# Mixing layers of a two-stack transformer kernel: VectorE's weight splits moved behind the maxima, ScalarE's split apart from them, and two scores put ahead of two value products

## What is computed

```python
h = rms_norm(x, attn_norm[l])
proj = h @ w_in[l]                       # 1024 x 2720, in column blocks of 256
o_a = neighborhood_attention(...)        # 4 heads, bias per row
o_b = diff_attention(...)                # 4 heads, two softmaxes each: p1 - lam * p2, then rms_norm
o_c = dilated_attention(...)             # 4 heads, bias
o_d = mla_attention(...)                 # 4 heads, 96 features
x = x + concatenate([o_a, o_b, o_c, o_d]) @ w_o[l]
```

## Time and profile before

| | |
|---|---|
| median of 3 runs | 1145.87 us (1145.69 to 1145.92) |
| the profiled execution's own time | 1145.93 us |
| its span, first to last instruction | 1143.9 us |
| TensorE busy | 1130.8 us, 99% of the span |
| VectorE busy | 778.2 us, 68% |
| ScalarE busy | 535.6 us, 47% |
| TensorE's granted clock, mean | 0.998 |

### The profile page before, as it was taken

One profiled execution on the slowest core, in us unless ns is written; L12 is line 12 of the kernel. 1 busy time (PEld: TensorE's weight loads), 2 busy tenths in 40 slices (PEclk: granted clock), 3 DMA queues, 4 the chain that ended last, 5 costly groups with the idle time before them and its releaser, 6 DMA issues. The chain is left out here.

```text
span 1143.9 us, 17037 instructions
## 1 busy us (share of the span) xinstructions
PE 1130.8 (99%) x6662; PEld 982.6 (86%) x6662; DVE 778.2 (68%) x999; ACT 535.6 (47%) x704; POOL 32.8 (3%) x47
## 2 busy tenths in 40 slices
PE   9999999999999999999999999999999999999997
PEld 7888888898888888879988888888899888888886
DVE  6766666766667666677686676666766866766665
ACT  5533333456653333344576543343446755433332
POOL 0000000000000000003000000000030000000000
PEclk9999999999999999999999999999999999999999
DMA  8765556764346555658423465556673243665550
GB/s 277 243 208 198 179 204 200 225 201 148 111 166 221 185 193 181 212 146 268 147 100 111 166 221 183 185 184 209 178 232 111 75 136 127 218 207 196 182 186 37
DMA packets 167131, 204.57 MB, mean 179 GB/s; under 512 B 19988, under 2 KB 150028, under 8 KB 167078
## 3 DMA queue, kind: packets, MB, share of 16 engines
q1 hardware_dynamic: 166606, 203.11, 54.6%
q10 hardware_dynamic: 472, 0.73, 0.2%
HBM read 202.66 MB, written 1.16 MB: 178 GB/s over the span
## 5 line engine op out<-in xcount | busy, mean ns | idle before, releaser
L628 ACT ACTIVATE whi<-raw 128x2048 fp32r<-128x2048 f32 x176 | 336.4, 1914 | 382.7 <-PE bank L1516 245.5
L949 DVE TENSOR_TENSOR wlo<-raw,whi 128x2048 fp32r<-128x2048 f32 x171 | 391.9, 2293 | 163.4 <-ACT whi L628 163.3
L1512 PE MATMUL bank<-h_both,whi 128*128 128x512 f32 x1280 | 304.6, 390 | 0.0
L1512 PEld LDWEIGHTS bank<-h_both,whi 128*128 128x128 f32 x1280 | 237.7, 188 | 47.7
L1486 PE MATMUL bank<-whi,o_hi 128*128 128x512 f32 x448 | 176.3, 393 | 0.0
L1487 PE MATMUL bank<-wlo,o_hi 128*128 128x512 f32 x448 | 174.9, 390 | 0.0
L1488 PE MATMUL bank<-whi,o_lo 128*128 128x512 f32 x448 | 174.4, 389 | 0.0
L1516 PEld LDWEIGHTS bank<-h_both,wlo 128*128 128x128 f32 x1280 | 164.1, 191 | 6.2
L1516 PE MATMUL bank<-h_both,wlo 128*128 128x256 f32 x1280 | 166.0, 283 | 0.0
L1488 PEld LDWEIGHTS bank<-whi,o_lo 128*128 128x128 f32 x448 | 84.1, 188 | 17.9
L1486 PEld LDWEIGHTS bank<-whi,o_hi 128*128 128x128 f32 x448 | 84.3, 188 | 17.6 <-issue 1.3
(11 more groups left out here) (179 smaller groups left out, 1172.6 us busy)
## 6 DMA issues: line engine op xcount, KB each, us to landing
raw<-in_w_gate_up SPq DMA_DIRECT2D x44, 1024.0 KB, 5.0
raw<-in_w_down SPq DMA_DIRECT2D x44, 1024.0 KB, 4.8
raw<-in_w_gate SPq DMA_DIRECT2D x22, 1024.0 KB, 5.1
raw<-in_w_up SPq DMA_DIRECT2D x22, 1024.0 KB, 5.1
raw<-in_w_in SPq DMA_DIRECT2D x20, 1024.0 KB, 6.2
raw<-in_w_o SPq DMA_DIRECT2D x12, 1024.0 KB, 4.8
raw<-in_w_kv SPq DMA_DIRECT2D x8, 1024.0 KB, 5.4
raw<-in_w_q SPq DMA_DIRECT2D x4, 1024.0 KB, 5.4
```

The costliest lines, as they stand in the source:

```text
L628: act.activation(whi[:, s, :], raw[:, s, :], ACT.Copy).then_inc(hi_ready, 1)
L949: dve.tensor_tensor(wlo[:, s, :], raw[:, s, :], whi[:, s, :].bitcast(F32), ALU.subtract).then_inc(lo_ready, 1)
L1512: pe.matmul(bank[bk + jj][:, :], hi[:, kc, jj * P:(jj + 1) * P], h_both[:, kc, :, :].rearrange("p a t -> p (a t)"), start=(kc == 0), stop= ...
```

## The change

In the list of events of a mixing layer, splits 9, 10 and 11 are taken apart into `hi n` (ScalarE's part) and `lo n` (VectorE's part).

- `hi 9` and `hi 10` stay where the splits stood, behind units 7 and 8. `lo 9` moves behind the maxima of items 8 and 9, `lo 10` behind those of items 12 and 13, each ahead of the normalisations of the same items.
- `hi 11` moves from behind unit 9 to behind the transposes of heads 10 and 11, and `lo 11` behind the differential heads' sums.
- The scores of items 16 and 17 (`scores`, on TensorE and VectorE) move ahead of the values of heads 10 and 11; their exponentials (`exps`, on ScalarE) come behind `diff_stats`, and their normalisations behind `diff_norm`.

```diff
-    s += TH(2, 3) + S(4, 5) + N(4, 5) + V(0, 1, 2, 3) + [("O", 0)] + S(6, 7) + N(6, 7) + unit(7)
-    s += TH(4, 5) + S(8, 9) + N(8, 9) + TH(6, 7) + V(4, 5) + S(10, 11) + N(10, 11) + unit(8)
-    s += TH(8, 9) + S(12, 13) + N(12, 13) + V(6, 7) + [("O", 1)] + V(8, 9) + S(14, 15) + N(14, 15) + unit(9)
-    s += TH(10, 11) + V(10, 11) + [("diff_stats",)] + S(16, 17) + N(16, 17) + [("diff_norm",)] + unit(10)
+    s += TH(2, 3) + S(4, 5) + N(4, 5) + V(0, 1, 2, 3) + [("O", 0)] + S(6, 7) + N(6, 7) + [("unit", 7), ("hi", 9), ("proj", 7)]
+    s += TH(4, 5) + S(8, 9) + [("lo", 9)] + N(8, 9) + TH(6, 7) + V(4, 5) + S(10, 11) + N(10, 11) + [("unit", 8), ("hi", 10), ("proj", 8)]
+    s += TH(8, 9) + S(12, 13) + [("lo", 10)] + N(12, 13) + V(6, 7) + [("O", 1)] + V(8, 9) + S(14, 15) + N(14, 15) + [("unit", 9), ("proj", 9)]
+    s += TH(10, 11) + [("hi", 11), ("scores", 16), ("scores", 17)] + V(10, 11) + [("diff_stats",), ("exps", 16), ("exps", 17), ("lo", 11), ("diff_norm",)]
+    s += N(16, 17) + unit(10)
...
-                    if k == "split":
+                    if k in ("split", "hi"):
                         split(u0 + ev[1])
...
-                    elif k == "S":
+                    elif k in ("S", "exps"):
                         exps(i0 + ev[1], ev[1], ev[1] >= 4)
...
-                    if k == "split" and ev[1] < 16:
+                    if k in ("split", "lo") and ev[1] < 16:
                         split(u0 + ev[1])
...
-                    elif k == "S":
+                    elif k in ("S", "scores"):
                         i = ev[1]
```

## The result

The changed kernel takes **1149.76 us** (median of 7 runs, 1149.58 to 1150.82), the kernel before in the same session 1145.92 us (7 runs, 1145.56 to 1147.12). The ratio is 1.0033, 95% interval 1.0024 to 1.0042: **slower by 3.8 us**, 1.9 in each mixing layer, and above the forecast's upper end of 1148.6. The profiled execution has a span of 1147.6 us (before 1143.9) and a mean granted clock of 0.998, as before.

What follows compares the result with a forecast made beforehand. TensorE, 99% busy, was taken as the bound; -0.44 + 0.72 + 0.43 = +0.71 us a layer, +1.4 in both, on 1145.87 gave 1147.3 us, range 1145.0 to 1148.6.

Steps and rivals of the forecast that it cites:

- beyond 3 us: Sign for the whole kernel: a difference beyond 3 us would mean a wait the prediction had not seen at all.
- What bounds the kernel: TensorE, 99% busy, bounds it; work moved on other engines counts only by what it makes TensorE wait for.
- The scores: S 16 and S 17 ahead of V 10 and V 11 remove TensorE's hole there: -0.44 us a layer.
- `lo 9` and `lo 10`: Splits behind maxima delay normalisations: T 9 waits for N 11, +0.72 us a layer; T 11 for N 15, +0.43.
- The far row: Item 4's row: an idle VectorE begins maxima 1.27 us after their scores start; applied to maxima 8 and 12.
- rival 1: Maxima come soon enough at T 9 and T 11, only the hole goes: -0.88 to -0.2 us; chance 0.17.
- `hi 11`, `lo 11`, and what is behind: Unit 11 needs `lo 11` some 5 us after it is made and later weight loads have room: cost nothing.
- rival 2: Late split 12 and `hi 13` delay T 13's copy for V 13: 2.3 us, up to 1148.9; chance 0.16.
- line 1791: Sign of rival 2: line 1791 or 1795 waits for `pt` longer than before.
- rival 3: S 16 takes over V 10's wait while T 9 and T 11 wait: +2.3 us at most, 1148.2; chance 0.04.
- rival 4: TensorE's clock falls in the new waits: 6 us more a layer at half clock, 1159; chance 0.01.
- The loads: SyncE's loads of units 12 to 14 leave about 3.4 to 6 us later but have room: cost nothing.

Runs made afterwards that it cites:

- experiment 1: Against the kernel before, only scores 16 and 17 moved ahead of V 10 and V 11, all splits as before; 1144.63 us, ratio 0.9993.
- experiment 9: Against experiment 4, split 9 put back whole behind unit 7, so of the early splits only `lo 10` is late; 1145.47 us, ratio 0.9996.
- experiment 4: Against the changed kernel, `lo 11` moved ahead of `diff_stats`, N 16 and N 17 back ahead of `diff_norm`; 1146.70 us, ratio 1.0008.
- experiment 5: Against the changed kernel, `lo 11` moved behind `diff_norm`; 1150.11 us, ratio 1.0038.
- experiment 3: Against the changed kernel, unit 9 with split 11 and the line of T 10 and T 11 as before; 1148.85 us, ratio 1.0029.
- experiment 7: Against experiment 1, the values of head 12 put between the transposes of heads 13 and 14; 1146.32 us, ratio 1.0005.
- experiment 8: Against experiment 1, the transposes of head 13 moved beside T 12, ahead of unit 11; 1144.70 us, ratio 0.9992.
- experiment 2: Against the changed kernel, splits 9 and 10 put back as before; 1147.45 us, ratio 1.0015.
- experiment 6: Against the changed kernel, `hi 13` moved behind ScalarE's copies of T 13 and T 14; 1147.65 us, ratio 1.0018.

## Why the prediction was wrong, point by point

The medians make a ladder, in us for both layers:

| step | from, to | difference | forecast |
|---|---|---|---|
| scores ahead of the values | 1145.77, 1144.63 | -1.1 | -0.88 |
| `lo 10` late (`hi 11` behind the transposes, `lo 11` ahead of the sums) | 1144.63, 1145.47 | +0.8 | +0.86 |
| `lo 9` late | 1145.47, 1146.70 | +1.2 | +1.44 |
| `lo 11` beside the power, N 16 and N 17 behind `diff_norm` | 1146.70, 1149.76 | +3.1 | 0 |

The first three rows sum to +0.9 for a forecast of +1.4; the fourth is the miss. The prediction had set a sign for it: beyond 3 us there would be a wait that it had not seen at all.

**What bounds the kernel: right.** The busy sums of VectorE and ScalarE stay within 1 us of before, and the time moved by what TensorE waited for or did less tightly.

**The scores: right.** The hole is gone and S 16 follows T 11 at once. From T 10 to unit 10 it is 3.86 us in experiment 1 (602.85 to 606.71) for 4.40 in the earlier trace rows: 0.54 a layer, the 1.1 of the medians, for a forecast of 0.44.

**`lo 9` and `lo 10`: right, in mechanism and nearly in size.** The far row held: maxima 8 started 1.26 us behind their scores with VectorE idle (580.78 to 582.04), maxima 12 1.16 (592.52 to 593.68), for the 1.27 of the earlier trace rows. That decided against rival 1. At T 9 the distance grew by 0.74 for a forecast of 0.72 (the bracket shows 0.51 of it), at T 11 by 0.34 for 0.43. In the ladder the first is 1.2 by the medians of experiments 9 and 4 and 1.5 by their profiled spans (1143.2 and 1144.7).

**The failed step: "`hi 11`, `lo 11`, and what is behind ... Cost nothing", and with it rival 2's sum, by which split 12 starts at 613.95.** There I let `diff_norm` follow `lo 11` at once, with GpSimd's power taken to be over by then. `lo 11` itself was 0.37 earlier than forecast (609.29 for 609.66), but then VectorE stood idle for 1.54 and split 12 came at 615.17: 613.95 - 0.37 + 1.54 = 615.12, so this one term is the whole miss of that start. The power beside a split takes 3.62 us. With VectorE idle (experiment 5), at maxima (before and experiment 3) or at normalisations (1, 4, 7, 8 and 9) it takes 1.64 or 1.65. The 3.62 shows in each of the three kernels that start `lo 11` beside the power (the changed one, experiments 2 and 6) and in no other, with the early splits late or not. It ends 1.51 behind the split: the power does nearly all of its work once the split is over, and is not merely slowed by it.

The price stood in the trace of the kernel before, in the same layer, where GpSimd adds a mask in eight operations of one shape and one split falls among them. The prediction did not use it:

```profile
537.65 0.73 POOL L590 TENSOR_TENSOR bias<-bias,nmask 128x256 f32<-128x256 f32 x1
537.88 2.65 DVE L949 TENSOR_TENSOR wlo<-raw,whi 128x2048 fp32r<-128x2048 f32 x1 [3.07 <-ACT whi L628]
538.34 2.77 POOL L590 TENSOR_TENSOR bias<-bias,nmask 128x256 f32<-128x256 f32 x1
```

The first of these additions is running when the split starts, and the split takes 2.65 for its usual 2.29: it ends 2.15 behind the end of that addition (538.38 to 540.53). The next addition takes 2.77 for 0.73 and ends 0.58 behind the end of the split. In both directions the later of the two ends as if it had begun some 0.14 or 0.15 ahead of the other's end. By that the power, started 0.18 behind `lo 11`, comes to 2.29 - 0.18 - 0.14 + 1.64 = 3.61 us, an estimate from these rows; 3.62 was measured.

The Trainium skill has this in "SBUF — State Buffer", section "SBUF: two separate sides": whichever of the two starts first, a VectorE operation with two inputs from SBUF or a GpSimd operation that reads SBUF, keeps the port pair that both share for the whole instruction, and the other is blocked. The split reads `raw` and `whi` from SBUF, and the traces agree: 3.62 against 1.64 with the split first, 2.65 against 2.29 with GpSimd first.

**Rival 2 was the right one, for a reason I did not have, and its price was too small.** I gave it 0.16, with the words that `hi 13` would end at 622.00 against a copy wanted at 622.07, and that each tenth later is lost one for one. `hi 13` ended at 623.20. The chain was right: split 12, maxima 18, `hi 13`, copy of T 13; and its sign, line 1791 (now 1792) waiting for `pt` longer than before, came true. Its highest price was 1148.9, outside the stated range and still below what was measured. "One for one" was not: the listed wait is 0.18 a layer, and putting the copy first (experiment 6) gives back 1.06 by the medians (0.94 by the pair's own time, 2.27 against 1.33), because with the wait heads 12 and 13 no longer run side by side. The rest of the 3.1 is `diff_T`, 0.47 a layer (T 13 starts at 621.49 in experiment 6 and at 621.02 in experiment 4), of which 0.25 stand in a bracket. 2 x (1.06 + 0.47) = 3.06, the first term by the medians, the second by the starts in the first layer. That all of this is the power's is worked out and not tested: no run frees the power and leaves the order. By the rows, without the 1.54 `hi 13` would end at 621.66 and, with `diff_T` not held either, the copy be wanted at about 621.65 (0.63 behind T 13, as before), just as the prediction had it.

**Rivals 3 and 4** did not happen in the changed kernel. Experiment 3 has rival 3's combination, the early splits with V 10 still waiting, and costs 3.1 where 2.3 were given, since V 10 waits longer behind the late `hi 11` (from T 10 to V 10 it is 2.09, for 1.40 before, of which 0.34 are T 11's wait). The clock was the same in all runs (mean granted 0.997 to 0.999). The stretch that the prediction read for rival 4 (820 to 840 us) does not hold the longest standstill: that one, 2.07 us, ends at 513.39, and from 511 to 516 us the granted clock is 1.00 as well, so the argument stands.

**The loads: right.** In the changed kernel's list of waits neither ScalarE nor VectorE waits for a load of the output product's weights (units 11 to 14).

The version to keep is that of experiment 1, which is 1.1 us below before and 5.1 below the changed kernel by the medians; against before its interval (0.9984 to 1.0002) reaches just over 1, so that gain is likely and not shown.

## What to carry to other kernels

Before a VectorE operation with two large inputs in SBUF is put into a wait for GpSimd, price GpSimd's operation as if it only began when VectorE's ends; and look in the trace at hand for a GpSimd operation whose time differs from its like. And where two matmul groups overlap on TensorE, the price of a wait between them is the wait and their overlap, so read distances from start to start rather than the list of waits.

## What the runs showed of the hardware

- GpSimd's 128 x 8 power of 1.64 us takes 3.62 beside VectorE's 2.29 us subtraction of two float32 tiles in SBUF, in all three kernels that have them together; beside VectorE's normalisations with one tile as input (experiment 4) it keeps its 1.64. In the kernel before, GpSimd's 128 x 256 addition takes 2.77 for 0.73 behind the start of such a subtraction, and the subtraction takes 2.65 for 2.29 when it starts during an addition.
- Products with a 64-wide output, whose two heads write rows 0 to 63 and 64 to 127 of the same PSUM bank (`rows` in `head_out`), run side by side: 1.0 us for one head alone (experiment 7), 1.03 for two that are both ready (experiment 8), 1.33 with the second head's copy half a microsecond behind (experiment 1), 2.27 when it is later still. The Trainium skill's "TensorEngine Tiling (Array Packing)", section Key Properties, says that different tiles of the array can load and multiply in parallel; the traces agree for two halves of 64 columns.
- An idle VectorE begins maxima 1.16 to 1.27 us after the start of the two items' scores, in three places (maxima 8, maxima 12), the scores themselves taking 1.14 of it.
